# A five-layer transformer stack on one core: the first two input products taken before the modulation's shift is known, the shift's share added afterwards

## The chip, the core and the metric

One NeuronCore of a Trainium2 chip runs the whole program. The metric is the device time of one execution in microseconds (us), median of the runs.

## What is computed

The reference runs four layers (sliding-window attention "swa", gated linear attention "gla", forgetting attention "fox", swa again), a final norm, and a fifth layer ("b2", differential attention) on one sequence of 256 tokens with 1024 features. Each layer begins like this, and only this place is touched, in layer 0:

```python
mod = c_act @ w_ada + b_ada          # c_act = silu(c), 1024 numbers; six parts of 1024
shift1, scale1, gate1, shift2, scale2, gate2 = split(mod, 6)
h = rmsnorm(x, g) * (1 + scale1) + shift1
proj = h @ w_in                      # 1024 x 1536 in the first layer
q, k, v = split(proj, ...)           # then rope on q and k, attention, output product
```

## The kernel before

**Tiling.** Features lie on the 128 partitions in C = 8 chunks `c`, tokens along the columns: `X`, `XN`, `hhi` and `hlo` are 128 x 8 x 256. Weights come in units of 1 MB (128 x 2048, which is 256 output columns for all 8 chunks) into six slots `raw`. Nearly all products are split: a weight unit is divided into a high part (ACT, `hi`, L999, `whi`) and a low part (DVE, `lo`, L1498, `wlo`), the activations likewise into `hhi` (ACT) and `hlo` (DVE), and TensorE makes three products for each pair. Only the first two units of layer 0 (`whole_pair`, L2188) and its output units are multiplied whole in fp32, straight out of `raw`; each such product shows as two records.

**The modulation.** It is no product on TensorE. `w_ada` comes in half units of 1 MB. DVE multiplies each with the broadcast `c_act` (`CB`) and sums the rows (`ada_sum`, L1523, two instructions for each half unit, each counted in `ada_dot`); `ada_add` (L1529) adds the bias and writes four columns of `MOD`. A unit `a` gives 4 of the 8 columns of a part: units 0 and 1 are shift1, units 2 and 3 are scale1. `affine` (L1543) makes gain * (1 + scale) from the latter.

**The start.** SP issues all loads by hand, in the order c, parameters `PAR`, half units 0 and 1 of `w_ada` into `adar`, half units 2 to 5 into slots 2 to 5 of `raw` (with the constants ones and identity, `CST`, between them), `X`, half units 6 and 7 into `adar` again, weight units 0 and 1, unit 2, the second part of `CST` (512 KB: cos, sin, perm, masks), `w16` (128 KB, a narrow weight of a later layer), units 3 to 5. Meanwhile ACT squares `X` (L1021), TensorE sums the squares over the features (L2205), ACT takes the root (L1006, L1007), and DVE scales (`XN`, L1577). ACT adds shift1 to `XN` (L1073), on which `whole_pair` works; then ACT makes `hhi` (L1076), DVE `hlo` (L1581), and DVE computes the few numbers `lam` (L1646 to L1654). Behind that both engines go through a list written out by hand: ACT splits unit 2 (L999) and `w16` (`w16hi`, L1218, which waits for `w16` and for the second part of `CST`), then copies the two banks of products out for the rope (`rope_read`, L1113); DVE makes `w16lo` (L1765), the low half of unit 2, `ada_all(4)`, the low half of unit 3, the rope of both, the low half of unit 4, `mask_max(0)` and so on (L1706). TensorE multiplies units 2 to 5 (L2125, L2104), the rope's turning products (L2261), scores (L2281) and transposes (L2308) between them. POOL normalises probabilities (L942, L943) and issues the later half units of `w_ada` on its own DMA queue (`first_ada`, L948), the first when `ada_dot` is 14, the second when it is 16.

Of the kernel before, what the change touches and what calls it, by code (L numbers as in the profile page):

```python
# [34 lines left out]
P = 128  # L35
# [104 lines left out]
def program(nc, weights, ada, c_in, x_in, cst_in, par_in, w16_in, onehot_in, rows, scratch, out, kinds=KINDS):  # L140
# [4 lines left out]
    with ctx:  # L145
# [44 lines left out]
        onehot = alo[0:32, 0, :]  # L190
        V = XN[:].rearrange("p c s -> p (c s)").rearrange("p (t n) -> p t n", t=2)
# [49 lines left out]
        norm_whole = sem("first_norm_whole")  # L241
# [37 lines left out]
        LOOP_ADA = [ADA_UNITS * (l + 1) - (2 if l < 2 else 0) for l in range(L)]  # L279

# [520 lines left out]
        def _(sp):  # L801
# [30 lines left out]
            sp.dma_start(PAR[:, 0:PAR_NOW], par_in[:, 0:PAR_NOW]).then_inc(par_in_s, 16)  # L832
            for h in range(2):
                sp.dma_start(adar[:, h, :], ada[h:h + 1].rearrange("a p n -> p (a n)")).then_inc(ada_in[h], 16)
            for k in range(4):
                sp.dma_start(raw[:, 2 + k, :], ada[2 + k:3 + k].rearrange("a p n -> p (a n)")).then_inc(ada_early[k], 16)
                if k == 1:
                    sp.dma_start(CST[:, 0:2 * P], cst_in[:, 0:2 * P]).then_inc(cst_in_s, 16)
            sp.dma_start(X[:], x_in).then_inc(x_in_s, 16)
            for h in range(2):  # L840
                sp.wait_ge(ada_dot, 2 * (h + 1))
                sp.dma_start(adar[:, h, :], ada[6 + h:7 + h].rearrange("a p n -> p (a n)")).then_inc(ada_in[h], 16)
            load_unit(0)
            load_unit(1)
            sp.wait_ge(ada_dot, 6)
            load_unit(2)
            sp.dma_start(CST[:, 2 * P:CST_NOW], cst_in[:, 2 * P:CST_NOW]).then_inc(cst2_in_s, 16)
            sp.dma_start(SCR[:, 4, 0:2 * P], w16_in).then_inc(w16_in_s, 16)
            for k in range(3, 6):
# [131 lines left out]
        def _(act):  # L981
# [81 lines left out]
            def norm(n, l=None, which=0):  # L1063
# [34 lines left out]
            for l, kind in enumerate(kinds):  # L1098
# [387 lines left out]
        def _(v):  # L1486
# [49 lines left out]
            def ada_read(a):  # L1536
                ada_add(a, a % 2, 4 * a)

            def affine(l, which):

                v.wait_ge(ada_mod, ADA_UNITS * l + (3 if which == 0 else 9) + 1)
# [27 lines left out]

            def norm(n, l=None, which=0):  # L1570
# [3 lines left out]

                if n == 0:
                    for k in range(C):
                        v.scalar_tensor_tensor(out=XN[:, k, :], in0=X[:, k, :], scalar=AFF[:, 0, k:k + 1], in1=RB[:, 1, :],  # L1577
                                               op0=ALU.mult, op1=ALU.mult).then_inc(norm_h, 1)
                    for k in range(C):
                        v.wait_ge(norm_hi, k + 1)  # L1580
                        v.tensor_tensor(hlo[:, k, :], XN[:, k, :], hhi[:, k, :].bitcast(F32), ALU.subtract).then_inc(norm_lo, 1)  # L1581
                    return
# [5 lines left out]
                for k in range(C):  # L1588
                    v.scalar_tensor_tensor(out=XN[:, k, :], in0=X[:, k, :], scalar=AFF[:, which, k:k + 1], in1=RB[:, 1, :],
                                           op0=ALU.mult, op1=ALU.mult).then_inc(norm_h, 1)  # L1590
                    if k >= 2:
                        low(k - 2)
                low(C - 2)
# [37 lines left out]
            for a in range(4):  # L1631
                ada_all(a)
                if a >= 1:
                    ada_read(a - 1)
            ada_read(3)

            for l, kind in enumerate(kinds):
# [6 lines left out]
                elif has_b2:  # L1644
                    v.wait_ge(pro_act, 1)
                    link(v.tensor_tensor(lam[:, 4:5], lam[:, 3:4], lam[:, 2:3], ALU.subtract))  # L1646
                    link(v.tensor_scalar(lam[:, 5:6], lam[:, 4:5], -LAMBDA_INIT, None, ALU.add))

                    link(v.tensor_scalar(lam[:, 4:5], lam[:, 5:6], -1.0, 1.0, ALU.mult, ALU.max))
                    link(v.tensor_tensor(lam[:, 4:5], lam[:, 4:5], lam[:, 5:6], ALU.max))  # L1650
                    link(v.reciprocal(lam[:, 6:7], lam[:, 4:5]))
                    link(v.tensor_tensor(lam[:, 7:8], lam[:, 6:7], lam[:, 5:6], ALU.mult))
                    link(v.tensor_scalar(epsd[:], lam[:, 6:7], lam[:, 6:7], EPS, ALU.mult, ALU.mult))
# [1159 lines left out]
```

## Time and profile before

| | |
|---|---|
| median of 3 runs | 1567.69 us (1567.59 to 1567.73) |
| the profiled execution | 1567.71 us, of which the span of the trace is 1565.9 us |
| instructions in the span | 24611 |
| TensorE matmul busy | 1531.1 us, 98% |
| TensorE weight load busy | 1320.0 us, 84% |
| DVE busy | 1185.9 us, 76% |
| ACT busy | 796.4 us, 51% |
| POOL busy | 107.7 us, 7% |
| the chain that ended last | TensorE 92%, DVE 4%, DMA 2%, ACT 1%, POOL 1% |

Busy shares are means over the whole span. The chain is followed back from the last instruction, at each step to what released it; it says which engine sets the end in each stretch. A row of the timeline gives start, duration, engine, line of the kernel and operation, output and inputs, and in brackets the idle time of the engine just before it with what ended it. The columns of a window are its bounds, its length, then busy time and number of instructions of each engine, the clock granted to TensorE (1.00 is 2.4 GHz, 0.50 is 1.2 GHz), the busy share of the DMA engines and GB/s.

### The profile page before, as it was taken

To read this page: it belongs to the slowest core of one execution; us is meant where nothing else is said; L and a number is where in the kernel's file an instruction comes from. 1 tells how busy PE (TensorE), PEld (TensorE's weight loads), DVE (VectorE), ACT (ScalarE), POOL (GpSimd) and SP (SyncE) were. 2 spreads that over 40 slices of the span, in tenths; PEclk is the share of its full clock that TensorE was granted. 3 is DMA by queue.
4 is the path that set the end of the run, shared out by engine and by line. 5 is a ranking of instruction groups with operands and counts; after the bars stand their busy time and mean duration, and the time that the engine had idled before them with its cause. 6 is when DMAs were issued, how large, how long until landed. Compare 5 with 4: busy or idle time off the path is not lost.

```text
span 1565.9 us, 24611 instructions
## 1 busy us (share of the span) xinstructions
PE 1531.1 (98%) x9327; PEld 1320.0 (84%) x9327; DVE 1185.9 (76%) x1775; ACT 796.4 (51%) x1100; POOL 107.7 (7%) x111
## 2 busy tenths in 40 slices
PE   4989999999999999999999999999999999999999
PEld 3868888899988888998888888888888888899998
DVE  7888877779488777855687777869777788676666
ACT  3455434465664434655544335665344677664544
POOL 0140000000000000011000000210000064200000
PEclk9999999999999999999999999999999999999999
DMA  9957788855169887663398885347888555345550
GB/s 388 385 186 270 304 326 328 338 192 209 55 241 381 306 329 279 262 217 127 144 379 317 308 310 199 138 162 305 338 302 323 210 186 178 119 166 193 179 188 28
DMA packets 55056, 383.28 MB, mean 245 GB/s; under 512 B 6437, under 2 KB 7077, under 8 KB 9538
## 3 DMA queue, kind: packets, MB, share of 16 engines
q1 hardware_dynamic: 51122, 363.23, 61.8%
q0 software_dynamic: 3856, 18.97, 3.4%
q8 instruction: 54, 0.88, 0.2%
q14 instruction: 24, 0.20, 0.0%
HBM read 381.10 MB, written 4.22 MB: 246 GB/s over the span
## 4 chain that ended last, share of the span: by engine, by line
PE 92%; DVE 4%; DMA 2%; ACT 1%; issue 1%; POOL 1%; SPq 0%; ACTq 0%; DVEq 0%
PE PS L2567 31%; PE PS L2104 26%; PE PS L2623 17%; PE PS L2125 5%; PE PS L2281 2%; PE PS L2356 2%; DMA raw<-weights 1%; PE PS L2331 1%; PE PS L2601 1%; DVE adar L1523 1%; PE PS L2308 1%; PE PS L2188 1%; PE PS L2261 1%; PE PS L2205 1%; DVE SCR L1706 1%
## 5 line engine op out<-in xcount | busy, mean ns | idle before, releaser
L1498 DVE TENSOR_TENSOR wlo<-raw,whi 128x2048 fp32r<-128x2048 f32 x223 | 512.2, 2298 | 134.7 <-ACT whi L999 134.4
L999 ACT ACTIVATE whi<-raw 128x2048 fp32r<-128x2048 f32 x228 | 434.8, 1911 | 180.5 <-PE PS L2623 116.1
L2104 PE MATMUL PS<-hhi,whi 128*128 128x256 f32 x1012 | 292.2, 289 | 0.0
L2104 PE MATMUL PS<-hhi,wlo 128*128 128x256 f32 x1012 | 286.9, 283 | 0.0
L2104 PE MATMUL PS<-hlo,whi 128*128 128x256 f32 x1012 | 286.9, 283 | 0.0
L1523 DVE CUSTOM_DVE_ANT_0 adar<-adar,CB 128x1024 f32<-128x1024 f32 x232 | 276.2, 1231 | 9.3 <-DMA adar<-ada 9.1
L2567 PE MATMUL PS<-whi,hhi 128*128 128x512 f32 x704 | 279.9, 398 | 0.9 <-ACT hhi L1045 0.9
L2567 PE MATMUL PS<-whi,hlo 128*128 128x512 f32 x704 | 274.7, 390 | 0.0
L2567 PE MATMUL PS<-wlo,hhi 128*128 128x512 f32 x704 | 274.4, 390 | 0.0
L2104 PEld LDWEIGHTS PS<-hhi,whi 128*128 128x128 f32 x1012 | 194.6, 192 | 6.6 <-issue 5.4
L2104 PEld LDWEIGHTS PS<-hlo,whi 128*128 128x128 f32 x1012 | 194.7, 192 | 1.7 <-issue 1.2
L2104 PEld LDWEIGHTS PS<-hhi,wlo 128*128 128x128 f32 x1012 | 194.6, 192 | 0.0
L2567 PEld LDWEIGHTS PS<-whi,hhi 128*128 128x128 f32 x704 | 132.2, 188 | 33.2 <-issue 2.8
L2623 PE MATMUL PS<-whi,ahi 128*128 128x512 f32 x400 | 156.2, 391 | 0.9 <-DVE wlo L1498 0.9
L2567 PEld LDWEIGHTS PS<-whi,hlo 128*128 128x128 f32 x704 | 132.1, 188 | 28.5
L2623 PE MATMUL PS<-whi,alo 128*128 128x512 f32 x400 | 155.7, 389 | 0.0
L2623 PE MATMUL PS<-wlo,ahi 128*128 128x512 f32 x400 | 155.7, 389 | 0.0
L2567 PEld LDWEIGHTS PS<-wlo,hhi 128*128 128x128 f32 x704 | 132.4, 188 | 25.8
L1444 ACT ACTIVATE ahi<-PS 128x512 fp32r<-128x512 f32 x44 | 26.4, 599 | 154.3 <-PE PS L2601 154.3
L1435 ACT ACTIVATE SCR<-PS 128x512 f32<-128x512 f32 x44 | 26.4, 600 | 128.4 <-PE PS L2567 128.4
L2045 DVE TENSOR_TENSOR alo<-PS,ahi 128x512 fp32r<-128x512 f32 x44 | 30.4, 691 | 79.3 <-ACT ahi L1444 79.3
L2623 PEld LDWEIGHTS PS<-whi,ahi 128*128 128x128 f32 x400 | 75.1, 188 | 16.3 <-issue 1.1
(280 smaller groups left out, 2133.4 us busy)
## 6 DMA issues: line engine op xcount, KB each, us to landing
raw<-weights SPq DMA_DIRECT2D x234, 1024.0 KB, 6.8
adar<-ada SPq DMA_DIRECT2D x104, 1024.0 KB, 5.2
adar<-ada POOLq DMA_DIRECT2D x12, 1024.0 KB, 6.4
raw<-ada SPq DMA_DIRECT2D x4, 1024.0 KB, 12.1
bias_rows<-bias_of_distance POOLq DMA_DIRECT2D x1, 3072.0 KB, 18.2
adar<-bias_rows POOLq DMA_DIRECT2D x8, 256.0 KB, 3.3
X<-x_in SPq DMA_DIRECT2D x1, 1024.0 KB, 16.7
adar<-bias_rows POOLq DMA_DIRECT2D x8, 128.0 KB, 2.7
```

The lines of the kernel that those rows point to most:

```text
L999: act.activation(whi[:, u % CV, :], raw[:, u % RAW, :], ACT.Copy).then_inc(hi_done, 1)
L1435: act.activation(two(SCR[:, 2, :]), row_banks(s_)[:, :, 0:S], ACT.Silu).then_inc(sg_done, 1)
L1444: act.activation(ahi[:, s_ % 2, :], src, ACT.Copy).then_inc(ahi_done, 1)
L1498: v.tensor_tensor(wlo[:, u % CV, :], raw[:, u % RAW, :], whi[:, u % CV, :].bitcast(F32), ALU.subtract).then_inc(lo_done, 1)
L1523: v.tensor_tensor_reduce(out=w, in0=w, in1=CB[:], scale=1.0, scalar=0.0, op0=ALU.mult, op1=ALU.add, accum_out=AS[:, par_, 2 * h + j:2 * h ...
L2045: v.tensor_tensor(alo[:, s_ % 2, :], src, ahi[:, s_ % 2, :].bitcast(F32), ALU.subtract).then_inc(alo_done, 1)
L2104: m = pe.matmul(o, w(a), h(b), start=first and k_ == 0, stop=last and k_ == 2, skip_group_check=True)
L2125: m = pe.matmul(o, hs[x][:, c, P * t:P * t + P], wt(a), start=(c == 0 and k_ == 0), stop=(c == C - 1 and k_ == 2))
L2281: m = pe.matmul(part(h, q), QT[r, p, P * q:P * q + P], KT[r, kt, 0:n], start=q == 0, stop=kind != "fox", skip_group_check=True)
L2356: return pe.matmul(o, raw[:, u % RAW, UC * p + P * part:UC * p + P * part + P], QT[:, p, :], start=first, stop=last, skip_group_check=True)
L2567: m = pe.matmul(row_banks(s_)[:, t, :], hs[x][:, c, P * t:P * t + P], ws[a][:, u % CV, 512 * (c % 4):512 * (c % 4) + 512], start=first and ...
L2623: m = pe.matmul(down_rows(t, h)[:], acts[x][:, s_ % 2, S * j + P * t:S * j + P * t + P], ws[a][:, u % CV, D * j + 512 * h:D * j + 512 * h ...
```

## The change

Two things move. The loads of `w_ada` for scale1 (units 2 and 3) come first, `X` and the constants ahead of them, and weight units 0 and 1 come before the loads for shift1 (units 0 and 1). And `whole_pair` multiplies the two weight units with the scaled `XN`, without the shift; when shift1 is there, the same weight tiles are multiplied with one column of it for each of the 4 output tiles (2 units, 2 halves) and 8 chunks, into banks 3 and 7, and ACT adds that column as a bias while it copies a bank out. `XN + shift` is never written: ACT makes `hhi` as XN + shift with one instruction for each chunk, DVE `hlo` with another. The pieces of the diff stand in the order definitions, SP, ACT, DVE, TensorE.

```diff
+        shift_cols = RB[:, 0, S - 4:S]
...
+        def first_of(a):
+            return (2, 3, 0, 1)[a]
...
+            sp.dma_start(CST[:, 0:2 * P], cst_in[:, 0:2 * P]).then_inc(cst_in_s, 16)
+            sp.dma_start(X[:], x_in).then_inc(x_in_s, 16)
+            def first_half(dst, k, done):
+                k = 2 * first_of(k // 2) + k % 2
+                sp.dma_start(dst, ada[k:k + 1].rearrange("a p n -> p (a n)")).then_inc(done, 16)
             for h in range(2):
+                first_half(adar[:, h, :], h, ada_in[h])
+            for k in range(2):
+                first_half(raw[:, 2 + k, :], 2 + k, ada_early[k])
+            load_unit(0)
+            load_unit(1)
+            for k in range(2, 4):
+                first_half(raw[:, 2 + k, :], 2 + k, ada_early[k])
             for h in range(2):
                 sp.wait_ge(ada_dot, 2 * (h + 1))
+                first_half(adar[:, h, :], 6 + h, ada_in[h])
+            for k in range(2, 6):
                 sp.wait_ge(ada_dot, 2 * (k + 1))
                 load_unit(k)
+                if k == 3:
+                    sp.dma_start(SCR[:, 4, 0:2 * P], w16_in).then_inc(w16_in_s, 16)
+                    sp.dma_start(CST[:, 2 * P:CST_NOW], cst_in[:, 2 * P:CST_NOW]).then_inc(cst2_in_s, 16)
...
                 if n == 0:
-                    for k in range(C):
-                        act.wait_ge(norm_h, k + 1)
-                        act.activation(XN[:, k, :], XN[:, k, :], ACT.Identity, bias=MOD[:, k:k + 1]).then_inc(norm_whole, 1)
-                    for k in range(C):
-                        act.wait_ge(norm_whole, k + 1)
-                        act.activation(hhi[:, k, :], XN[:, k, :], ACT.Copy).then_inc(norm_hi, 1)
-                elif n != plan.final_norm:
+                    act.wait_ge(ada_mod, 4)
+                if n != plan.final_norm:
...
                 def unit_read(i, dst, scale=1.0):
                     act.wait_ge(pe_unit, u0 + i + 1)
+                    if l == 0 and i < 2:
+                        link(act.activation(shift_cols[:, 2 * i:2 * i + 2], bank[(3, 7)[i]][:, 0:2], ACT.Copy))
+                        for t in range(2):
+                            e = act.activation(dst[:, t, :], bank[i][:, S * t:S * t + S], ACT.Identity, bias=shift_cols[:, 2 * i + t:2 * i + t + 1])
+                        e.then_inc(bank_read, 1)
+                        return
...
+                if n == 0:
+                    lambdas()
+                    ada_all(2)
+                    ada_read(2)
+                    ada_all(3)
+                    ada_read(3)
+                    v.wait_ge(ada_mod, 4)
+                    for k in range(C - 2):
+                        low(k)
...
-                idle_products(8, 0)
-                pe.wait_ge(ada_dot, 16)
+                for n in (4, 6, 8):
+                    idle_products(7, 0)
+                    pe.wait_ge(ada_dot, n)
                 idle_products(3, 0)
+                for b in (0, 1, 3, 7):
+                    if b == 3:
+                        pe.wait_ge(norm_r, 1)
+                    pe.matmul(bank[b][:], zeros[:], zeros[:, 0:1].to_broadcast([16, 512]), start=True, stop=True)
                 for b in range(2):
                     pe.wait_ge(raw_in[b], 16)
-                for c in range(C):
-                    pe.wait_ge(norm_whole, c + 1)
-                    for b in range(2):
+                    for c in range(C):
+                        pe.wait_ge(norm_h, c + 1)
...
+                pe.wait_ge(ada_mod, 4)
+                for b in range(2):
+                    for t in range(2):
+                        for c in range(C):
+                            m = pe.matmul(bank[(3, 7)[b]][:, t:t + 1], raw[:, b, UC * c + P * t:UC * c + P * t + P], MOD[:, c:c + 1],
                                           start=False, stop=c == C - 1, skip_group_check=True)
+                    m.then_inc(pe_unit, 1)
```

How the instructions stand, without any time. A row is line, operation, output, inputs, shape, what it waits for, and how many alike follow each other. First SP's queue from its second load on, before:

```order
L832 DMA PAR<-par_in 128x173
L834 DMA adar<-ada 128x2048 x2
L836 DMA raw<-ada 128x2048 x2
L838 DMA CST<-cst_in 128x256
L836 DMA raw<-ada 128x2048 x2
L839 DMA X<-x_in 128x2048
L842 DMA adar<-ada 128x2048 [waits ada_rows_dotted] x2
L817 DMA raw<-weights 128x2048 x2
L817 DMA raw<-weights 128x2048 [waits ada_rows_dotted]
L847 DMA CST<-cst_in 128x1024
L848 DMA SCR<-w16_in 128x256
```

and the same stretch now (`ada` is the modulation's weight, `ada_rows_dotted` the count `ada_dot`):

```order
L837 DMA CST<-cst_in 128x256
L838 DMA X<-x_in 128x2048
L843 DMA adar<-ada 128x2048 x2
L843 DMA raw<-ada 128x2048 x2
L821 DMA raw<-weights 128x2048 x2
L843 DMA raw<-ada 128x2048 x2
L843 DMA adar<-ada 128x2048 [waits ada_rows_dotted] x2
L821 DMA raw<-weights 128x2048 [waits ada_rows_dotted] x2
L860 DMA SCR<-w16_in 128x256
L861 DMA CST<-cst_in 128x1024
```

`X` and weight units 0 and 1 move ahead; `w16` and the second part of `CST` now stand behind one more weight unit, unit 3.

TensorE between the second weight unit's last whole product and unit 2, now (`MOD` holds shift1, `ada_ready` counts the sums of `ada_add`):

```order
L2204 MATMUL PS<-XN,raw 128x256 [waits norm_scaled]
L2204 MATMUL PS<-XN,raw 128x256
L2210 MATMUL PS<-MOD,raw 128x1 [waits ada_ready]
L2210 MATMUL PS<-MOD,raw 128x1 x31
L2138 MATMUL PS<-whi,hhi 128x256 [waits norm_lo,cst_first_layer_loaded,lo_split]
```

Before, the product of unit 2 followed the whole products directly; now 32 products of one column stand between them, the first of which waits for all of shift1.

## Rows read from the trace of the kernel before

**Rows 1.** The chain that ended last, in order of time: start us, us, what

```profile
1.57 5.19 DMA adar<-ada
...
12.54 19.76 DMA raw<-weights
...
32.34 14.08 PE PS L2188 x64
46.42 2.87 PE PS L2125 x24
...
68.34 0.66 PE PS L2308 x6
...
69.89 0.35 DVE SCR L1706
```

**Rows 2.** The timeline of DVE: start us, us, line, op, count [idle before <-releaser]

```profile
6.91 1.23 DVE L1523 CUSTOM_DVE_ANT_0 adar<-adar,CB 128x1024 f32<-128x1024 f32 x1 [3.13 <-DMA adar<-ada]
...
24.56 1.23 DVE L1523 CUSTOM_DVE_ANT_0 adar<-adar,CB 128x1024 f32<-128x1024 f32 x1 [2.51 <-DMA adar<-ada]
...
25.71 1.22 DVE L1523 CUSTOM_DVE_ANT_0 adar<-adar,CB 128x1024 f32<-128x1024 f32 x1
...
29.94 3.26 DVE L1577 SCALAR_TENSOR_TENSOR XN<-X,AFF,RB 128x256 f32<-128x256 f32 x8
...
36.79 0.15 DVE L1646 TENSOR_TENSOR lam<-lam 128x1 f32<-128x1 f32 x1
...
42.25 0.43 DVE L1765 TENSOR_TENSOR w16lo<-SCR,w16hi 128x256 fp32r<-128x256 f32 x1 [3.90 <-ACT w16hi L1218]
42.59 2.29 DVE L1498 TENSOR_TENSOR wlo<-raw,whi 128x2048 fp32r<-128x2048 f32 x1
...
65.56 0.15 DVE L1725 TENSOR_TENSOR RB<-RB 128x4 f32<-128x4 f32 x1
...
69.89 0.35 DVE L1706 CUSTOM_DVE_ANT_0 SCR<-PS,CST,nsink 128x128 f32<-128x128 f32 x1 [0.95 <-PE PS L2281]
```

**Rows 3.** The timeline of ACT, same columns

```profile
22.15 2.28 ACT L1021 ACTIVATE XN<-X 128x512 f32<-128x512 f32 x5 [6.72 <-DMA X<-x_in]
...
33.67 2.54 ACT L1076 ACTIVATE hhi<-XN 128x256 fp32r<-128x256 f32 x8
...
41.70 0.42 ACT L1218 ACTIVATE w16hi<-SCR 128x256 fp32r<-128x256 f32 x1 [2.27 <-DMA SCR<-w_in]
45.60 0.60 ACT L1113 ACTIVATE SCR<-PS 128x512 f32<-128x512 f32 x1 [3.48 <-PE PS L2188]
```

**Rows 4.** The timeline of POOL, same columns

```profile
27.24 0.72 POOL L948 DMA_DIRECT2D adar<-ada  x1 [26.80 <-DVE AS L1523]
...
66.95 1.03 POOL L943 TENSOR_TENSOR SCR<-SCR,RB 128x512 f32<-128x512 f32 x1
```

**Rows 5.** POOL's DMA queue from 28 to 32 us: packets, MB, share of engines

```profile
q0 software_dynamic: 27, 0.22, 13.2%
```

**Rows 6.** Both DMA queues (POOL's q0, SP's q1) from 36 to 40 us

```profile
q0 software_dynamic: 150, 1.06, 63.5%
q1 hardware_dynamic: 216, 0.59, 37.6%
```

**Rows 7.** The chain from 393 to 404 us: products with few columns

```profile
394.37 3.77 PE PS L731 x32
398.13 5.31 PE PS L740 x48
```

**Rows 8.** The timeline of PE: start us, us, line, op, count [idle before]

```profile
14.64 0.59 PE L2225 MATMUL PS<-lam,CST 128*128 128x2 f32 x2 [8.67 <-DMA CST<-cst_in]
22.83 5.39 PE L2205 MATMUL PS<-XN,CST 128*128 128x256 f32 x16 [7.61 <-ACT XN L1021]
```

**Rows 9.** Windows: span us, busy us of PE, PEld, DVE, ACT, POOL, PEclk, DMA

```profile
90.00:95.00 5.00, 2.70 (x22) 1.94 (x19) 4.93 (x16) 2.38 (x9) 4.50 (x4) 0.95 0.61 208
95.00:98.00 3.00, 3.00 (x12) 2.08 (x12) 1.96 (x4) 1.96 (x10) 3.00 (x3) 0.51 0.78 314
```

More of the change, by code:

```diff
@@ L1536, in ada_read @@
             def ada_read(a):
-                ada_add(a, a % 2, 4 * a)
+                ada_add(a, a % 2, 4 * (first_of(a) if a < 4 else a))
             def affine(l, which):
-                v.wait_ge(ada_mod, ADA_UNITS * l + (3 if which == 0 else 9) + 1)
+                v.wait_ge(ada_mod, ADA_UNITS * l + (3 if which == 0 else 9) + 1 if l or which else 2)
                 sc = MOD[:, 48 * l + 8 + 24 * which:48 * l + 16 + 24 * which]
@@ L1568, in add_squares, with lambdas @@
                 v.tensor_tensor(XN[:, a, :], XN[:, a, :], XN[:, b, :], ALU.add).then_inc(norm_add, 1)
+            def lambdas():
+                if has_b2:
+                    v.wait_ge(pro_act, 1)
+                    link(v.tensor_tensor(lam[:, 4:5], lam[:, 3:4], lam[:, 2:3], ALU.subtract))
+                    link(v.tensor_scalar(lam[:, 5:6], lam[:, 4:5], -LAMBDA_INIT, None, ALU.add))
+                    link(v.tensor_scalar(lam[:, 4:5], lam[:, 5:6], -1.0, 1.0, ALU.mult, ALU.max))
+                    link(v.tensor_tensor(lam[:, 4:5], lam[:, 4:5], lam[:, 5:6], ALU.max))
+                    link(v.reciprocal(lam[:, 6:7], lam[:, 4:5]))
+                    link(v.tensor_tensor(lam[:, 7:8], lam[:, 6:7], lam[:, 5:6], ALU.mult))
+                    link(v.tensor_scalar(epsd[:], lam[:, 6:7], lam[:, 6:7], EPS, ALU.mult, ALU.mult))
+                    link(v.tensor_scalar(epsd[:], epsd[:], 1e-36, None, ALU.max))
             def norm(n, l=None, which=0):
                 v.wait_ge(norm_r, n + (plan.final_norm is None or n < plan.final_norm))
[L1575 to L1582, printed above, removed]
                 def low(k):
@@ L1590, in norm @@
                                            op0=ALU.mult, op1=ALU.mult).then_inc(norm_h, 1)
-                    if k >= 2:
+                    if k >= 2 and n:
                         low(k - 2)
+                if n == 0:
[7 more added lines that the diff above has]
+                        low(k)
                 low(C - 2)
@@ L1630, in _ @@
             v.wait_ge(c_act, 1)
[L1631 to L1635, printed above, removed]
+            ada_all(0)
+            ada_all(1)
+            ada_read(0)
+            ada_read(1)
             for l, kind in enumerate(kinds):
@@ L1643, in _ @@
                     ada_read(LOOP_ADA[l - 1] + 10)
[L1644 to L1653, printed above, removed]
-                    link(v.tensor_scalar(epsd[:], epsd[:], 1e-36, None, ALU.max))
                 u0 = plan.uin[l]
@@ L2176, in whole_pair @@
             def whole_pair():
[L2178 to L2179 removed]
+                for n in (4, 6, 8):
+                    idle_products(7, 0)
+                    pe.wait_ge(ada_dot, n)
                 idle_products(3, 0)
+                for b in (0, 1, 3, 7):
+                    if b == 3:
+                        pe.wait_ge(norm_r, 1)
+                    pe.matmul(bank[b][:], zeros[:], zeros[:, 0:1].to_broadcast([16, 512]), start=True, stop=True)
                 for b in range(2):
[L2182 removed]
                     pe.wait_ge(raw_in[b], 16)
[L2184 to L2186 removed]
+                    for c in range(C):
+                        pe.wait_ge(norm_h, c + 1)
                         for t in range(2):
[L2188 removed]
+                            pe.matmul(bank[b][:, S * t:S * t + S], raw[:, b, UC * c + P * t:UC * c + P * t + P], XN[:, c, :],
+                                      start=False, stop=c == C - 1, skip_group_check=True)
+                pe.wait_ge(ada_mod, 4)
[3 more added lines that the diff above has]
+                            m = pe.matmul(bank[(3, 7)[b]][:, t:t + 1], raw[:, b, UC * c + P * t:UC * c + P * t + P], MOD[:, c:c + 1],
                                           start=False, stop=c == C - 1, skip_group_check=True)
[L2190 to L2191 removed]
+                    m.then_inc(pe_unit, 1)
             def sum_squares(n):
```

19 lines of the change are left out of this document (removed).

## Prediction

> **What bounds the kernel now.** I read the page's summary first: TensorE holds 92% of the chain, so only the few places where it waits can give anything, and this change touches only the start. Then the chain in order of time [rows 1]. The reader is to see three stretches. Up to 32.3 us DMA sets the pace: the chain's transfer `raw<-weights` ends at 12.54 + 19.76 = 32.30, and the whole products start at 32.34. From there to 69.87 it is all TensorE, the whole products taking 14.08 us and the product of unit 2 starting at 46.42. At 69.89 the chain passes to DVE (`mask_max(2)`).
>
> The chain names only the last of several near rivals, so the timelines come next. DVE [rows 2] is as important: it waits 3.90 us until 42.25 for `w16hi`, and from 42.25 on it has no gap until shortly before 69.89, where it waited 0.95 us for TensorE. ACT [rows 3] shows what that wait was: `w16hi` started at 41.70 when a DMA landed. So two chains run side by side from 42 to 70, TensorE's and DVE's. DVE's starts with **a DMA landing at 41.7**, not with the products.
>
> **The new timetable of the loads.** The DMA engines are saturated at the start. From the first half unit (used at 6.91) to `X` (used at 22.15) [rows 2, 3] 6.125 MB landed: five half units, 128 KB of constants and `X`. That is 15.24 / 6.125 = 2.49 us for each MB; with 1.08 MB up to 6.91, a load lands at 4.2 + 2.49 x (MB up to its end). `X` now ends at 1.21 MB, so 7.2. The four half units of scale1 end with 5.21 MB at 17.2, weight units 0 and 1 at 19.7 and 22.2, the four of shift1 at 24.6, 27.1, 29.6 and 32.1, units 2 and 3 at 34.6 and 37.1.
>
> **The first products.** A half unit costs DVE 2.4 us (from 24.56 to 25.71 + 1.22 [rows 2]), so scale1's last is summed at 19.6. The sums' addition and `affine` take 0.6, scaling starts at 20.2 and lasts 3.26 [rows 2]. The sum of squares started 0.7 us after ACT's first square and took 5.39 [rows 3, 8]; from `X` at 7.2, with 2 us allowed for what stands ahead on ACT, that is 15.3, and with every record at half clock (16 of twice 0.22) 16.9; the root behind it is covered. TensorE has 3 idle products and 4 clearing ones to make after 19.6, some 1.3 us. Whole products run from 20.9 to 20.9 + 14.1 = 35.0; unit 1 (22.2) is not waited for, since unit 0 takes 7 us alone.
>
> **The shift.** DVE ends scaling at 23.4, computes `lam` (36.79 until the idle time of 3.90 before 42.25 begins, 1.6 us [rows 2]) until 25.0, then sums the shift's half units until 27.4, 29.8, 32.2 and 34.6; with the addition shift1 is ready at 34.8, just ahead of the whole products' end. Then 32 products of one column, 64 records. The trace has no such product in a row. The nearest are weight tiles of 128 x 128 with 64 columns, 5.31 / 48 = 0.111 us a record, and with 128 columns, 3.77 / 32 = 0.118 [rows 7]: halving the columns hardly changes it, so the weight load sets it. Bounds: 0.111 and the whole product's 14.08 / 64 = 0.22 [rows 1]. I take 0.11, so 64 x 0.11 = 7.0 us, and the products end at 42.0 instead of 46.42: 4.4 us earlier. The Trainium skill, "TensorE: Matmul & The Clock Gate", section "Back-to-back issue gap", lists about 60 cycles, 25 ns, for 1 to 64 columns, which would make the shift 1.6 us; the rows with 64 columns contradict that here, and neither value is waited for in my sum.
>
> **What then holds unit 2.** Its product needs `whi`, `wlo` of unit 2 and `hlo`. ACT makes `hhi` from 34.8 on in 2.54 to 3.3 us, then `whi` in 1.91: free at 40.0 at the latest. DVE's `hlo` (eight of the kind that took 3.26) ends at 38.5. Both then stand before the second part of `CST` and `w16`, behind which the low half of unit 2 is queued on DVE. Before, from landing to the end of that half it took 42.59 + 2.29 - 41.70 = 3.2 us. So the landing decides.
>
> It used to be 41.7 with 12.83 MB on SP's queue and POOL's two half units (2 MB) all ahead: 4.2 + 2.49 x 14.83 = 41.1. Now 13.83 MB are on SP's queue up to its end; without POOL that is 38.6. POOL issues its first at `ada_dot` 14: before, that was 27.24, 2.68 us after the seventh half unit's start [rows 2, 4]; now 29.8 + 2.7 = 32.5. Its bytes came some 3.7 us after the issue (0.22 MB by 32 us at about 0.2 MB per us [rows 5]), so now from 36.2. By then about 0.6 MB of SP's are still to flow, `w16` and `CST` in short pieces. In the stretch where just these pieces met POOL's, SP moved 0.59 MB in 4 us against POOL's 1.06 [rows 6]. That makes 40.2 for the flow and, with a landing some 1.1 us behind (38.6 against 37.5 for 0.6 MB from 36.2 at full rate), about 41.3 for the landing. Bounds: 38.6 (POOL never in the way; then ACT's 40.0 holds, gain 1.7) and 43.6 (all 2 MB in the way, loss 1.9). Nearest are the rows of the same pieces, so I take 41.3, **0.4 us earlier**. The Trainium skill, "DMA: Bandwidth & Descriptors", section "Queues, rings and completion order", has each engine change queues after a packet of some 9 to 17 descriptors; by that a group of POOL's long pieces (half of a 1 MB load's time of 5 us at a shared rate) would pass first and then the short ones as one group, with a landing near 41.6 as an estimate and a gain of 0.3 us less. The stretch at 36 to 40 us looks like piece by piece, with the long pieces getting 64% of the bytes.
>
> **The sum.** The low half of unit 2 ends at 41.3 + 3.2 = 44.5, so its product starts 1.9 us earlier than 46.42, though the operands from the shift were ready at 42.0; 2.5 of the 4.4 us won are lost in this wait. Two ACT copies become six instructions (two of 0.60 become two of a few columns and four of 256 columns, 0.42 each as `w16hi` [rows 3], with two waits for their own result): some 1.1 us more, before the high half of unit 3, in a stretch where ACT now is 2 us ahead. DVE's list has no gap from here, so it is only 0.4 us ahead. By 68 us TensorE needs POOL's probabilities: L943 ends at 66.95 + 1.03 = 67.98, after DVE's sums at 65.56 [rows 2, 4], and the transposes began at 68.34 [rows 1]; POOL follows DVE, so of TensorE's lead only 0.36 us less the hand-over of 0.12 is kept, 0.24. The gain that reaches `mask_max(2)` is 0.4 + 0.24 = 0.64 us. From 70 to 110 us DVE, POOL and TensorE hand work to each other in an unchanged order and carry it on. 1567.71 - 0.64 = 1567.07; the profiled execution is 0.02 above the median, so I say 1567.1 us. A measurement of this kernel can tell about 0.2%, 3.1 us, from no change.
>
> **Rivals.** (1) *The clock falls in the shift, partly.* The granted clock was 0.95 and then 0.51 after a stretch in which PE was busy 2.70 of 5 us [rows 9]. One-column products load weights but hardly multiply, and then TensorE idles 2.5 us. If that counts as idle, the last part of the shift runs at 0.22 instead of 0.11, ending near 45.3, and unit 2 begins at 1.2 GHz for one or two stretches like that of [rows 9], 1.5 to 3 us lost. Against it: the 64-column products of [rows 7] ran for 5 us at full pace. Against 46.42 that is 46.8 to 48.3, 0.4 to 1.9 us slower than before: 1568.1 to 1569.6. The same TensorE page, Part 1, says that the gate follows how busy PE is; it does not settle whether loads count.
> (2) *Slower for good: all of the shift at 1.2 GHz.* Two records of 2 columns at the slow clock took 0.59 us with 0.22 between them [rows 8]. 64 x 0.22 = 14.1, from 35.0 to 49.1, 2.7 us after 46.42, and 1.5 for a slow start of unit 2: 4.2 us slower, 1571.9. It decides if the clock is at half when the last whole product ends; these products fill the array, so it is unlikely.
> (3) *The constants land late.* POOL's bytes catch `w16` and all of `CST`: landing up to 43.6, DVE late, up to 1569.4. For it speaks that 128 KB of `w16` go in short pieces; against, that POOL starts as they finish.
> (4) *More is freed.* The landing at 40.0 or before (1.7 + 0.24 us), and the slow clock at 95 to 98 us, 3 us busy at half [rows 9], does not recur at the shifted times: 1.5 us. 1565.8 or 1565.6 (with the forecast's 0.64) by one alone, 1564.3 by both.
>
> **The numbers.** Forecast 0.56; rival 1 0.18; rival 2 0.04; rival 3 0.08; rival 4 0.14. Rival 4 passes 3.1 us only with both parts, so faster by over 0.2% has 0.05; slower has rival 2 and 0.02 for more slow stretches in rival 1, 0.06; the rest, 0.89, is within 0.2%. The range reaches from rival 4's single cases to rival 3's end and most of rival 1: 1565.3 to 1569.6.
>
> **What the changed profile would show.** Whole products from about 20.9 to 35.0; 64 short records at 0.11 until 42.0; a wait of TensorE for `wlo` of about 2.5 us; `w16hi` at 41.3; DVE nearly without a gap from there, `mask_max(2)` at about 69.2. Wrong, if `w16hi` starts outside 40.6 to 42.3, if the short records need 0.2 us each, or if the granted clock is below 1 between 36 and 50 us.

## The result, and the profile after

The changed kernel takes **1571.8 us** (median of 10 runs, 1569.3 to 1572.3) against 1567.6 us (10 runs); the ratio is 1.0025, 95% interval 1.0017 to 1.0033: slower by about 4 us. Forecast were 1567.1 us and no measurable difference, and the range ended at 1569.6. The profiled execution took 1571.63 us, its span 1569.7 (before: 1567.71 and 1565.9). Of the experiments below, one execution, of a_pool_late, took 1676.9 us at a lower granted clock and is left out of the medians.

The chain of the kernel after, in order of time (start us, us, what), against [rows 1]:

```profile
20.38 24.32 DMA CST<-cst_in
48.08 5.33 PE PS L2138 x24
55.12 2.87 PE PS L2138 x24
...
115.46 17.46 PE PS L2377 x80
```

From the first products on, the chain is no longer TensorE's but runs through the second part of `CST`, which lands at 20.38 + 24.32 = 44.70, to unit 2's product, whose first half takes 5.33 us where it took 2.87. Its timelines: TensorE, then DVE, ACT, POOL (start us, us, engine, line, op, ..., in brackets the idle time before and what ended it), against [rows 2 to 4, 8]:

```profile
21.28 14.08 PE L2204 MATMUL PS<-XN,raw 128*128 128x256 f32 x64
35.75 10.47 PE L2210 MATMUL PS<-MOD,raw 128*128 128x1 f32 x64 [0.39 <-DVE MOD L1540]
48.08 0.55 PE L2138 MATMUL PS<-whi,hhi 128*128 128x256 f32 x1 [1.85 <-DVE wlo L1509]
...
33.12 1.23 DVE L1534 CUSTOM_DVE_ANT_0 adar<-adar,CB 128x1024 f32<-128x1024 f32 x1 [1.14 <-DMA adar<-ada]
36.35 3.25 DVE L1602 SCALAR_TENSOR_TENSOR hlo<-XN,MOD,hhi 128x256 fp32r<-128x256 f32 x8 [0.65 <-ACT hhi L1085]
45.30 0.43 DVE L1778 TENSOR_TENSOR w16lo<-SCR,w16hi 128x256 fp32r<-128x256 f32 x1 [5.69 <-ACT w16hi L1229]
...
73.99 0.35 DVE L1719 CUSTOM_DVE_ANT_0 SCR<-PS,CST,nsink 128x128 f32<-128x128 f32 x1 [1.17 <-PE PS L2302]
...
35.73 3.30 ACT L1085 ACTIVATE hhi<-XN,MOD 128x256 fp32r<-128x256 f32 x8 [20.46 <-DVE MOD L1540]
38.95 1.89 ACT L1009 ACTIVATE whi<-raw 128x2048 fp32r<-128x2048 f32 x1
44.78 0.42 ACT L1229 ACTIVATE w16hi<-SCR 128x256 fp32r<-128x256 f32 x1 [3.95 <-DMA CST<-cst_in]
...
32.29 0.72 POOL L958 DMA_DIRECT2D adar<-ada  x1 [31.85 <-DVE AS L1534]
```

`w16hi` starts at 44.78 instead of 41.70 [rows 3], so DVE begins its list 3.1 us late. Unit 2's product starts 1.7 us late (48.08 against 46.42) and its first half takes 2.5 us longer. The 64 short records last 10.47 us, not 7.0. `mask_max(2)`, DVE's first L1719 with 1.17 us of idle time, is at 73.99 instead of 69.89 [rows 2]: 4.1 us late, which is the 1.7 and the 2.5 together. The windows of the kernel after show the second thing (us, length, busy of PE, PEld, DVE, ACT, POOL, then PEclk, DMA, GB/s):

```profile
35.75:39.50 3.75, 3.75 (x34) 3.75 (x34) 3.15 (x8) 3.75 (x9) 0.55 (x1) 0.99 1.02 414
39.50:46.20 6.70, 6.70 (x32) 6.64 (x32) 1.01 (x3) 2.65 (x5) 0.00 (x0) 0.50 1.02 421
46.20:48.00 1.80, 0.02 (x1) 0.00 (x0) 1.80 (x2) 1.71 (x4) 0.00 (x0) 0.50 1.03 428
48.00:53.20 5.20, 5.12 (x24) 5.16 (x25) 5.20 (x9) 2.91 (x2) 0.92 (x2) 0.51 1.01 421
53.20:58.00 4.80, 4.80 (x32) 3.84 (x31) 4.70 (x6) 0.00 (x0) 0.14 (x1) 1.00 1.01 416
```

The granted clock falls to 0.50 (1.2 GHz) at 39.5, 3.75 us after the first one-column product, and stays there until 53.2. That is one profiled execution, but the mean clock of a whole execution was 0.994 or 0.995 in all ten runs of the changed kernel, and 0.997 to 1.000 in 29 of the 30 runs of the kernel before that were counted beside the first experiments; 13.7 us at half clock make 0.004 of it. Until 39.5 a short record takes 3.75 / 34 = 0.11 us, then 6.70 / 32 = 0.21. The profile has TensorE fully busy in both windows.

From `mask_max(2)` to the 80 records that start at 115.46 (before: 110.89) the order is as before, and 0.5 us more are lost, which makes +4.6. The span is only 3.8 us longer, since a half-clock stretch of the kernel before at 347 us does not occur after; from those 80 records to the end it is 1454.2 us after, 1455.0 before.

So there were two suspects: **(A)** the constants land late, and **(B)** the clock is at half from 39.5 to 53.2.

### The profile page after: what moved, and what is told of

The parts are those of the page before. It is cut to its first block, busy times and chain, and to the rows that moved or that the text cites. A ratio compares the mean times of both kernels' runs of the same rounds, so it can differ in the third digit from the quotient of the medians.

```text
span 1569.7 us, 24758 instructions
## 1 busy us (share of the span) xinstructions
PE 1545.2 (98%) x9396; PEld 1332.7 (85%) x9406; DVE 1186.0 (76%) x1775; ACT 794.5 (51%) x1096; POOL 109.6 (7%) x111
## 4 chain that ended last, share of the span: by engine, by line
PE 88%; DVE 5%; DMA 2%; ACT 1%; issue 1%; POOL 1%; SPq 0%; ACTq 0%; DVEq 0%
PE PS L2588 31%; PE PS L2117 25%; PE PS L2644 17%; PE PS L2138 3%; PE PS L2302 2%; DMA CST<-cst_in 2%; PE PS L2377 1%; PE PS L2622 1%; PE PS L2352 1%; DVE wlo L1509 1%; PE PS L2329 1%; DMA raw<-ada 1%; PE PS L2282 1%; DVE adar L1534 1%; PE PS L2226 1%
## 6 DMA issues: line engine op xcount, KB each, us to landing
bias_rows<-bias_of_distance POOLq DMA_DIRECT2D x1, 3072.0 KB, 13.7
```

## The experiments

All were timed in 5 rounds beside the kernel before. The three last columns come from the profiled executions (us): start of `w16hi` on ACT, of unit 2's product on TensorE, and of `mask_max(2)` on DVE. The medians of the kernel before in the other rounds were 1566.4 to 1567.7 us, so the ratio, and not the difference of two medians of the table, compares like with like. Its interval is 1.3 to 1.6 us to either side (2.1 us for before_short1 and before_short64, which have five runs), and many of the outcomes told apart below differ by no more than that. They are told apart by the last three columns, and each of these is one execution. (Unit 2's start is the chain's, or the timeline's for a_pool_late; where nothing is waited for, the timeline's is some 0.15 us earlier.)

| kernel | median | ratio to before, 95% interval | w16hi | unit 2 | mask_max(2) |
|---|---|---|---|---|---|
| before | 1567.6 | | 41.70 | 46.42 | 69.89 |
| changed | 1571.8 | 1.0025 (1.0017 to 1.0033) | 44.78 | 48.08 | 73.99 |
| a_const_u2 | 1569.2 | 1.0009 (1.0000 to 1.0018) | 40.82 | 45.83 | 71.42 |
| b_wide64 | 1571.9 | 1.0027 (1.0017 to 1.0037) | 44.78 | 48.07 | 74.24 |
| b_wide64_fill | 1570.8 | 1.0018 (1.0009 to 1.0027) | 44.69 | 47.98 | 72.76 |
| ab_const_wide64 | 1568.2 | 0.9999 (0.9990 to 1.0008) | 40.96 | 44.23 | 70.97 |
| before_const_late | 1569.0 | 1.0012 (1.0003 to 1.0021) | 44.04 | 48.53 | 72.14 |
| before_short1 | 1578.3 | 1.0079 (1.0065 to 1.0093) | 41.69 | 56.95 | 81.93 |
| before_short64 | 1574.5 | 1.0044 (1.0031 to 1.0058) | 41.94 | 53.55 | 77.08 |
| a_pool_late | 1570.5 | 1.0019 (1.0010 to 1.0028) | 40.59 | 45.42 | 72.79 |
| f_onecol | 1569.9 | 1.0013 (1.0004 to 1.0022) | 46.61 | 45.64 | 71.26 |
| a_w16_u2 | 1570.7 | 1.0021 (1.0012 to 1.0030) | 42.97 | 46.27 | 71.64 |
| f_consts_free | **1566.3** | 0.9988 (0.9979 to 0.9997) | 44.91 | 43.41 | 68.58 |

**a_const_u2.** The constants behind unit 2, as their order was before:

```diff
-                if k == 3:
+                if k == 2:
                     sp.dma_start(SCR[:, 4, 0:2 * P], w16_in).then_inc(w16_in_s, 16)
```

> The changed kernel with one line moved: w16 and the second part of CST are loaded behind unit 2, not behind unit 3. My theory is that two losses make up the +4.1 us at mask_max(2): (A) the second part of CST lands at 44.8 instead of 41.7, so DVE starts its list 3.1 us late, and (B) TensorE runs at half clock from 39.5 to 53.2, which costs the one-column products 3.4 us and unit 2's product 2.5 us. Under A and B both: the constants land at 37 to 38.5, w16hi then waits only for ACT (40.9), the low half of unit 2 ends near 44.1 (3.8 us earlier than in the changed kernel), but the shift's products still end at 46.2, and unit 2's product begins there at half clock: mask_max(2) about 1.9 us earlier than in the changed kernel, 1569.8. A alone (the clock harmless, covered by DVE's lateness): 1567.9 or less. B alone (the landing harmless): unchanged, 1571.8.

1569.2 us, where both losses together gave 1569.8. `w16hi` waited for nothing but ACT, and the chain is then all TensorE's, short products and a slow unit 2:

```profile
35.83 10.00 PE PS L2210 x64
45.83 5.00 PE PS L2138 x24
```

A alone would have given 1567.9 or less, B alone no change. B alone is out by the time. Against A alone speaks the trace and not the time, whose interval (1567.5 to 1570.3) holds 1567.9 too: `mask_max(2)` is still 1.5 us late, with the constants there in time, and the clock is what is left.

**b_wide64.** The short products get 64 equal columns:

```diff
-pe.matmul(bank[(3, 7)[b]][:, t:t + 1], raw[...], MOD[:, c:c + 1],
+pe.matmul(bank[(3, 7)[b]][:, 64 * t:64 * t + 64], raw[...], MOD[:, c:c + 1].to_broadcast([P, 64]),
```

> The changed kernel with 64 equal columns of the shift in each of the short products instead of one; the loads stay. It asks whether the few columns let the clock fall. If they do (theory B): 64 records at 0.11 us, 7.1 us in all, ending at 42.9, with the granted clock at 1.00 throughout; then TensorE waits 5 us for the low half of unit 2 (47.9). Either the clock holds there, unit 2's product takes 2.9 us, and TensorE is 2.4 us earlier, of which DVE's lateness (+3.1 us) lets 1.0 us through: 1570.8; or it falls in this longer wait, and the time stays at 1571.8. If something else than the columns lets the clock fall (the weight loads themselves), it falls near 39.5 as before and nothing changes.

1571.9 us, the second of its two outcomes. Windows of b_wide64:

```profile
36.00:43.00 7.00, 7.00 (x64) 6.96 (x63) 3.25 (x8) 4.81 (x9) 0.34 (x1) 1.00 1.03 420
43.00:46.50 3.50, 0.09 (x1) 0.00 (x0) 1.20 (x2) 1.66 (x6) 0.00 (x0) 1.00 1.02 425
46.50:53.50 7.00, 5.43 (x25) 5.46 (x26) 7.00 (x10) 4.16 (x4) 1.06 (x2) 0.52 1.01 420
```

With 64 columns the clock stayed at 1.00 through all 64 records, 7.0 us in all, so few columns let it fall. It then fell in the wait for the constants, and unit 2 was as slow as ever: A brings B back.

**b_wide64_fill.** 64 columns, and behind them `idle_products(20, 5)`.

> As the kernel with 64 columns, and 20 idle products of 512 columns (some 4.4 us) behind them, up to the low half of unit 2. This takes loss B away altogether and leaves loss A. Theory of both: granted clock 1.00 from 36 to past 53 us, unit 2's product 2.9 us long from 48.1, mask_max(2) at +3.1 us against the kernel before instead of +4.1: 1570.8. B alone: 1567.7 or less. A alone: 1571.8, no change.

1570.8 us, as both losses gave; `mask_max(2)` is 2.9 us late, 3.1 were expected. The clock in the window of it:

```profile
36.00:54.00 18.00, 17.40 (x124) 13.88 (x124) 12.05 (x19) 10.57 (x18) 1.34 (x3) 1.00 1.02 419
```

B gone altogether gives back 1.2 us at `mask_max(2)`. The 2.9 us that are left go with a `w16hi` that is 3.0 us late.

**ab_const_wide64.** Both one-line edits.

> The constants behind unit 2 and 64 columns in the short products, both at once. Theory of both: short products end at 42.9, the low half of unit 2 at 44.1, unit 2's product begins near 44.2 at full clock, 1.9 us before that of the kernel before (46.42); DVE's list is 0.8 us earlier than before, so mask_max(2) comes 0.8 us earlier than before: 1566.9. If a part of the loss sits elsewhere (the order of the products, the six ACT copies), it stays above 1568.

1568.2 us, 1.3 more than expected, and not to be told from the kernel before. Unit 2 started 2.2 us earlier than before, and DVE's list 0.8 us earlier, but two new things came (DVE's timeline, then two windows):

```profile
48.25 1.23 DVE L1534 CUSTOM_DVE_ANT_0 adar<-adar,CB 128x1024 f32<-128x1024 f32 x1 [1.87 <-DMA adar<-ada]
...
36.00:44.50 8.50, 7.66 (x68) 7.55 (x67) 6.30 (x11) 7.29 (x17) 0.55 (x1) 1.00 1.01 420
44.50:48.00 3.50, 3.50 (x19) 3.50 (x18) 1.88 (x4) 2.67 (x2) 0.53 (x1) 0.52 1.01 419
```

DVE now waited 1.87 us for POOL's second half unit: 0.8 less 1.87 is the +1.1 seen at `mask_max(2)`. And the clock was at half from 44.5 to 48, though TensorE had waited only 0.84 us before 44.23; in b_wide64_fill, with idle products of 512 columns instead of a wait, it did not fall.

**before_const_late.** A in the kernel before: `CST` and `w16` behind unit 3.

> The kernel before with one thing changed: the second part of CST and w16 are loaded behind unit 3, not behind unit 2. It asks for loss A alone, with no short products anywhere. If the landing of the constants sets DVE's list, it moves from 41.7 by one unit of 1 MB, 2.5 us, to 44.2; the low half of unit 2 ends at 47.4 instead of 44.9, TensorE waits 1 us (too short for the clock to fall), and mask_max(2) and the end move by 2.5 us less nothing: 1570.1. If the landing is harmless (TensorE's lead covers it), the time stays at 1567.5 to 1568.5.

1569.0 us, 1.1 below the expected, and half a microsecond above what "harmless" gave, which the interval (1568.2 to 1571.0) doesn't exclude. The trace does: `w16hi` was at 44.04 and `mask_max(2)` 2.25 us late. In this execution the clock was at half early in the whole products, so TensorE was late as well; chain and window:

```profile
32.86 15.66 PE PS L2189 x64
48.53 2.87 PE PS L2126 x24
...
32.00:36.00 4.00, 3.14 (x7) 2.52 (x8) 3.10 (x10) 4.00 (x12) 0.00 (x0) 0.59 1.01 418
```

DVE's list began with `w16lo` at 44.59 (before: 42.25) and had no gap until shortly before `mask_max(2)`; that alone is 2.3 us. It reaches TensorE through POOL, whose L944 (L943 before) ends at 70.31 instead of 67.98, with the transposes right behind it, so A's price does not rest on TensorE's own lateness.

**before_short1 and before_short64.** B in the kernel before: 32 unused products added ahead of unit 2, with 1 and with 64 columns.

```diff
+                for b in range(2):
+                    for t in range(2):
+                        for c in range(C):
+                            pe.matmul(bank[(3, 7)[b]][:, 64 * t:64 * t + 1], CST[:, P * t:P * t + P], MOD[:, c:c + 1],
+                                      start=c == 0, stop=c == C - 1, skip_group_check=True)
```

> The kernel before with 32 products of one column added between the whole products and unit 2 (weight tiles are the constants in CST, the moving column is one of MOD; the result goes to banks 3 and 7 and is not used). No load moves. It prices loss B alone. Theory B: as in the changed kernel, full pace for some 3.7 us, then half clock, 64 records in 10.4 us instead of 7.1, and unit 2's product at half clock, 5.3 us instead of 2.9: the end moves by 10.4 + 2.4 = 12.8 us, 1580.3. If the fall of the clock in the changed kernel came from the wait behind the short products and not from them, the clock stays at 1.00 here, since nothing waits behind them: +7.1 us, 1574.6.

> As the kernel with 32 added products of one column, but each with 64 equal columns. If few columns are what lets the clock fall, the 64 records take 7.1 us at full clock, and unit 2's product follows at 2.9 us or at half clock for a part, since in the changed kernel with 64 columns and early constants the clock still fell, 1.4 us behind them: +7.1 to +8.8 us, 1574.6 to 1576.3. If the weight loads lower the clock whatever the columns, it is as slow as with one column: 1580.3.

Chain of before_short1, then of before_short64:

```profile
32.40 15.77 PE PS L2188 x64
48.17 8.78 PE PS L2195 x64
56.95 4.38 PE PS L2125 x24
```

```profile
32.37 14.08 PE PS L2188 x64
46.45 7.09 PE PS L2195 x64
53.55 2.93 PE PS L2125 x24
```

With 64 columns 7.09 us at full clock and 1574.5 us, as expected. With one column the clock fell with nothing waiting behind them, 4.9 us after their start, so the fall comes from the short products and not from the wait. It cost 1.69 us in them and 1.45 in unit 2, 3.1 together; I had expected 5.7, the size in the changed kernel, where it lasted 13.7 us and here 6.8. At `mask_max(2)` the two are 4.85 us apart: these 3.1, and 1.7 from a half-clock stretch in the whole products of before_short1 (15.77 us against 14.08), ahead of the added products. The medians are only 3.8 apart; the last section has a likely reason.

**a_pool_late.** `first_ada` waits for `max(16, ...)`: POOL's first transfer is issued 3.4 us later.

> The changed kernel with POOL's first transfer issued when ada_dot is 16 instead of 14, so both of its half units are issued near 35.8 and none near 32.3. SP's loads keep their order. It asks why the constants landed at 44.8 and not at the 41.3 forecast. My theory: POOL's bytes take 0.27 MB per us against SP's 0.13 in short pieces, and all 2 MB of them were ahead of the end of CST. Then most of unit 3, w16 and CST is through before POOL's bytes begin near 39.5, the second part of CST lands at 40.5 to 42.5, DVE's low half of unit 2 ends near 44.5, and TensorE (short products to 46.2 at half clock) sets unit 2's start as in the kernel with constants behind unit 2. ada_all(4) then waits for its half units until 45 to 47.5. Time 1569.2 to 1570.2. If POOL's transfers have nothing to do with it, and unit 3 and the constants are only late by SP's own order, the constants stay at 44.8 and the time at 1571.8 or above.

`w16hi` started at 40.59 with no wait: the constants were there. The two queues from 36 to 40 us (packets, MB, share of the engines), in a_pool_late, then in the changed kernel, whose first line also counts packets by size:

```profile
q1 hardware_dynamic: 395, 1.51, 94.4%
q0 software_dynamic: 16, 0.13, 7.9%
```

```profile
DMA packets 377, 1.65 MB, mean 412 GB/s; under 512 B 39, under 2 KB 152, under 8 KB 228
...
q0 software_dynamic: 151, 1.13, 68.4%
q1 hardware_dynamic: 226, 0.52, 33.4%
```

So POOL's two half units alone delay the constants from at most 40.6 to 44.8. The time is still 1570.5 us, 0.3 above the expected, since DVE then waited 1.38 and 2.58 us for those same half units: what one load wins on the engines, another loses.

**a_w16_u2.** Only `w16` ahead of unit 3.

> The changed kernel with only w16 (128 KB) loaded one place earlier, ahead of unit 3; the second part of CST stays behind unit 3. It asks how the two DMA queues share an engine while both have work. Theory of pieces: an engine takes one piece of each queue in turn. w16 is 8 pieces of 1 KB for each engine and the second part of CST 8 of 4 KB; in the changed kernel each waited for one of POOL's pieces of 8 KB (0.31 us), so these 16 pieces took 16 x 0.31 + 8 x (0.05 + 0.16) = 6.6 us from about 37. With w16 through before POOL's bytes begin, only the 8 pieces of CST alternate, 8 x (0.31 + 0.16) = 3.8 us from about 37, and with a landing about 1 us behind the flow CST lands at 41.5 to 42.3 instead of 44.8. Theory of bytes (my prediction's: so many MB ahead at so many MB per us): the same bytes are ahead of the end of CST, and it lands at 44.5 to 44.8 as before. Time by the first: w16hi near 42, the low half of unit 2 at 45.1, unit 2's product at 46.2 behind the short products at half clock, mask_max(2) 1.9 us earlier than in the changed kernel, 1569.2 to 1570; by the second 1571.8.

The constants came at 42.97, 1.8 us earlier, with the same bytes ahead of them. That excludes the count by bytes (44.5 to 44.8): the four executions with the changed kernel's order of loads and `w16hi` waiting for the landing have it at 44.69 to 44.91. The count by pieces gave the direction and 2.5 to 3.3 us of size; what is missing sits in a few engines, for most of the pieces of 4 KB (115 of 128) had gone by 39, and the last went just before 42. Why single engines lag was not tried. The time, 1570.7 us, is 0.7 above the expected 1569.2 to 1570.

**f_consts_free, the version that beats both.** The changed kernel's order of loads and 64 columns; unit 2 no longer stands behind the constants:

```diff
                     hi(u0 + 2)
                     if l == 0:
-                        act.wait_ge(w16_in_s, 16)
-                        act.wait_ge(cst2_in_s, 16)
-                        act.activation(w16hi[:].rearrange("p a b -> p (a b)"), SCR[:, 4, 0:2 * P], ACT.Copy).then_inc(pro_act, 1)
+                        hi(u0 + 3)
...
                     rope_read(0)
                     rope_read(1)
                     if l == 0:
-                        hi(u0 + 3)
+                        act.wait_ge(w16_in_s, 16)
+                        act.wait_ge(cst2_in_s, 16)
+                        act.activation(w16hi[:].rearrange("p a b -> p (a b)"), SCR[:, 4, 0:2 * P], ACT.Copy).then_inc(pro_act, 1)
                         hi(u0 + 4)
...
-                    pe.wait_ge(cst2_in_s, 16)
...
-                    unit(2, lambda: (aux_product(0), aux_product(1)))
+                    unit(2, lambda: (pe.wait_ge(cst2_in_s, 16) if l == 0 else None, aux_product(0), aux_product(1)))
```

and on DVE `w16lo`, with its two waits, moves from ahead of `lo(u0 + 2)` to behind `lo(u0 + 3)`, which itself moves ahead of `ada_all(4)`.

> A version meant to beat both: the changed kernel with its own order of loads and 64 columns in the short products, but nothing of unit 2 stands behind the constants any more: ACT splits unit 3 before w16 and copies the banks out before it, DVE makes the low halves of units 2 and 3 before w16lo, and TensorE waits for the constants only in the middle of unit 2, where it needs them. By my theory of both losses: the low half of unit 2 ends at 43.2, that of unit 3 at 45.4, ada_all(4) (whose half units land at 45.4) runs from 45.9 to 50.4 and the rope starts at 50.5 instead of 51.6 before: mask_max(2) 1.1 us earlier than before, 1566.4. If the clock still falls behind the short products, unit 2's product loses up to 1.7 us and TensorE, not DVE, is the later: 1566.4 to 1568.

1566.3 us, ratio 0.9988 (0.9979 to 0.9997): 1.9 us faster than before by the ratio (0.5 to 3.3), 1.4 by the medians of the same rounds, and 5.5 faster than the changed kernel. Its timelines and two windows:

```profile
40.97 4.49 DVE L1509 TENSOR_TENSOR wlo<-raw,whi 128x2048 fp32r<-128x2048 f32 x2 [1.25 <-ACT whi L1009]
68.58 0.35 DVE L1719 CUSTOM_DVE_ANT_0 SCR<-PS,CST,nsink 128x128 f32<-128x128 f32 x1 [0.87 <-PE PS L2301]
...
44.91 0.42 ACT L1236 ACTIVATE w16hi<-SCR 128x256 fp32r<-128x256 f32 x1 [0.31 <-DMA CST<-cst_in]
...
43.41 0.36 PE L2137 MATMUL PS<-whi,hhi 128*128 128x256 f32 x1 [0.19 <-DVE wlo L1509]
...
36.00:43.00 7.00, 7.00 (x64) 7.00 (x64) 5.29 (x9) 6.97 (x12) 0.47 (x1) 1.00 1.03 421
43.00:48.00 5.00, 4.81 (x31) 3.82 (x30) 5.00 (x6) 2.64 (x7) 0.00 (x0) 1.00 1.02 422
```

The constants land as late as ever (44.91), but nothing that matters waits for them, and the clock never falls there. One thing is not shown: the low half of unit 3 now also stands ahead of `ada_all(4)`, and this new order of ACT's and DVE's lists was never tried in the kernel before. How much of the 1.9 us belongs to the change and how much to the order of the lists is open.

**f_onecol.** The same with one column in the short products.

> The version whose unit 2 waits for no constants, but with one column in the short products as in the changed kernel. It is the second price of loss B with A cured, and it asks how much of that version's gain hangs on the 64 columns. Both losses: the short products fall to half clock near 39.6 and end at 46.2, unit 2's product follows without a wait and takes 5.3 us, so TensorE is 3.5 to 5 us behind the version with 64 columns at unit 3, of which the 1.4 us that it had waited for DVE and POOL come back: mask_max(2) near 71.5, time 1569 to 1570. If the low clock costs nothing once the constants are out of the way: 1566.3.

1569.9 us, as both losses gave; `mask_max(2)` at 71.26 against 71.5 expected. Chain:

```profile
35.70 9.94 PE PS L2209 x64
45.64 5.03 PE PS L2137 x24
```

So all of the gain hangs on the columns. The slow short products are felt twice here: ACT copies their bank out before it comes to `w16hi`, which starts at 46.61, though the constants are there. Four kernels now stand in a square, by `mask_max(2)` (before: 69.89):

| | unit 2 waits for the late constants | it does not |
|---|---|---|
| clock falls (1 column) | 73.99 (changed) | 71.26 (f_onecol) |
| clock holds (64 columns) | 72.76 (b_wide64_fill) | 68.58 (f_consts_free) |

Against the lower right corner the clock alone costs 2.7 us and the constants alone 4.2, but both together 5.4. (The columns differ in the order of the lists too, so the 4.2 has that in it.) That is less than the sum, 6.9, since unit 2 starts at 48 with the late constants whether the short products were slow or not: their 3.4 us are hidden in the wait. It is more than the larger one, since unit 2's product at half clock comes behind the wait: 2.5 us on TensorE's chain, of which DVE's lateness hides half. Curing the clock alone gives back 1.2 us, curing the constants alone 2.7.

## Why the prediction was wrong

**What held.** DMA set the pace up to the first products, and the timetable of the loads: whole products 21.28 to 35.36 (20.9 to 35.0 forecast), POOL's first issue at 32.29 (32.5). Shift1 was ready 0.9 us later than forecast (35.73 against 34.8), because the shift's last half unit landed about 1 us late (DVE waited 1.14 us for it, until 33.12). The pace of a short product at full clock was right: 0.11 us a record, with one column as with 64, and the weight loads fill all of the time (3.75 of 3.75 us until 39.5). Unit 2 did wait for the low half behind the constants, and the landing decided when. All three signs of being wrong that the prediction named came: `w16hi` at 44.78, short records of 0.21 us, a clock below 1 between 39.5 and 53.2.

**The first step that failed: the landing, forecast 41.3, measured 44.7.** The prediction priced what was left of SP's loads in bytes, with the SP share of [rows 6] (0.59 MB in 4 us against POOL's 1.06). But the two queues share an engine by pieces, whatever their size. From 37 to 39 us, in the changed kernel, POOL's pieces are 8 KB and SP's mostly 1 or 4 KB, and as many go of one as of the other (packets, MB, share of the engines):

```profile
q0 software_dynamic: 78, 0.64, 76.8%
q1 hardware_dynamic: 79, 0.18, 23.4%
```

And `w16` has as many pieces (one for each partition, 8 for each engine) as any load of 1 MB. In [rows 6] it stood last, where POOL's bytes ran out; the change moved it ahead of `CST`, into the thick of them. If each of the 16 short pieces of `w16` and `CST` on an engine has one of POOL's 8 KB pieces for company, 16 x 0.31 us of POOL's and 8 x (0.05 + 0.16) of their own are 6.6 us as an estimate, from about 37, and the landing follows about 1 us later: 44.6. That it meets the 44.7 so closely is in part luck. It holds for the slowest engines only: 102 of the 128 pieces of 4 KB had gone by 41, when POOL had moved 1.41 MB of its 2, and the last went just after 44. The landing (44.70) comes behind that last piece. Why a few engines lag by 3 us is open, as in a_w16_u2.

My worst case (43.6) took all of POOL's 2 MB and was right in that for the last pieces; it left out that SP's loads ran late, as the half unit above did by about 1 us. The Trainium skill, "DMA: Bandwidth & Descriptors", section "Queues, rings and completion order", has an engine change queues after some 9 to 17 descriptors; by that too, loads of 8 pieces for each engine count by number and not by bytes. No run here tells that from a change after every piece.

**The second: the short products' time, forecast 7.0 us, measured 10.5, and unit 2's product behind them at full clock.** They were priced at 0.11 us a record throughout. That holds at full clock, but the clock fell after 3.75 us, which cost 3.4 us in them and 2.5 in unit 2. The 3.4 are hidden in the wait for the constants; the 2.5 are not, and the sum had nothing for them. Rival 1 had this mechanism with 0.18, and its price (0.4 to 1.9 us slower than before) is about what the clock costs without the late constants: 1.6 us in a_const_u2, 2.2 in f_onecol. What misled was the evidence against it, 64-column products of [rows 7] at full pace for 5 us: true for 64 columns (b_wide64 shows it again), and no evidence for one. The Trainium skill, "TensorE: Matmul & The Clock Gate", Part 1, says that the gate follows how busy TensorE has been; here the profile had TensorE busy at 100% while the clock fell (3.75 of 3.75 us), so its busy share does not tell what the gate will do.

**The third: the range.** Rival 3 (constants late, 0.08) ended at 1569.4; alone, in b_wide64_fill, it came to 1570.8. Rival 1 ended at 1569.6. Both came true at once, which was not worked out: the constants set when unit 2's product starts and the clock how long it lasts, so one does not cover the other. Rival 2's time, 1571.9, is near the result only by its number: half clock through all of the shift did not occur.

**What cost nothing.** The 1.1 us more that ACT needs for its six copies do not show: ACT waited 7.18 us for TensorE before 58.08.

## What to carry over

Where two DMA queues meet, count the pieces of a load for each engine, not its bytes: moving the 128 KB of `w16` out of the way brought `CST` 1.8 us earlier, where its bytes at 2.49 us for each MB are worth 0.3. Products of one column let the clock fall even back to back with full weight loads; if the weight load sets their pace anyway, give them 64 equal columns. And when two things are late, price the pair: with one cured the other may hide the gain (b_wide64: 1571.9 us, no gain), and the first is not refuted by that.

## What the hardware did unexpectedly

The clock stayed at full through 64 records of 64 columns (7.09 us), and was at half 3.75 us (changed kernel) or 4.9 us (before_short1) after the first of one column. Nor is a stretch of 64 columns quite safe: in ab_const_wide64 it fell 1 us behind them after a wait of only 0.84 us (my expectation for before_const_late took 1 us for too short); in f_consts_free, with a wait of 0.19 us, it did not. What in few columns lets it fall is open; the runs show only that it does.

The times of one kernel lie in groups some 2 us apart (before_const_late: four of 1567.4 to 1567.7 us, seven of 1568.8 to 1571.0). The traces show a likely cause. In nine of the 13 profiled executions the clock is at half once between 93 and 106 us, and from `mask_max(2)` to the 80 records (at 110.89 in the kernel before) it takes 41.0 to 41.5 us. In the other four (before_const_late, before_short1, a_pool_late, a_w16_u2) it is not, and the same work takes 39.3 to 39.4; these four are among the quickest of their kernel's runs. Which way an execution goes was never steered, so this is read off, not shown. It also makes a median depend on how many of its runs went either way: before_short1's, 1578.3, is of the quick kind. That is why a difference of 1 to 2 us is better read at `mask_max(2)` than from the times.
